# Differential attention: the next head's maxima and exponentials stand ahead of this head's mixing and copy

## The reference

```python
def one_block(args):
    a1, a2, i = args
    q_chunk = (i * Q_BLOCK + jnp.arange(Q_BLOCK)) // CHUNK
    mask = (key_chunk[None, :] <= q_chunk[:, None])[None, None]
    s1 = jnp.einsum('bqhd,bkhd->bhqk', a1, k1) * scale
    s2 = jnp.einsum('bqhd,bkhd->bhqk', a2, k2) * scale
    p1 = jax.nn.softmax(jnp.where(mask, s1, -jnp.inf), axis=-1)
    p2 = jax.nn.softmax(jnp.where(mask, s2, -jnp.inf), axis=-1)
    p = (p1 - lam * p2)
    return jnp.einsum('bhqk,bkhe->bqhe', p, v)
...
o = rmsnorm_2(o, b_subln[j], SUBLN_EPS) * (1.0 - lam_init)
x = x + concat([o, memory_attention]) @ w_o[l]
```

## Time and profile before

| | before |
|---|---|
| median of 3 runs | 1191.41 us (1191.03 to 1191.85) |
| the profiled execution's own time | 1190.21 us |
| its span, first to last instruction | 1188.4 us |
| mean granted TensorE clock | 0.947 of full |
| PE busy | 1109.9 us (93%) |
| DVE busy | 641.9 us (54%) |
| ACT busy | 534.8 us (45%) |
| POOL busy | 356.4 us (30%) |
| stretch of the six heads, 918.09 to 964.04 us | 45.95 us, of it PE busy 32.55 us, granted clock 0.68 |

### The profile page before, as it was taken

The page is one execution under the profiler, slowest core; times in us unless marked ns, Lnnn a source line. Parts: engine busy times, 40 slices in busy tenths (PEclk is TensorE's granted clock), DMA queues, the critical chain, the costliest instruction groups (busy, mean ns, idle before and its releaser), DMA issues.

```text
span 1188.4 us, 20203 instructions
## 1 busy us (share of the span) xinstructions
PE 1109.9 (93%) x8758; PEld 1083.8 (91%) x8758; DVE 641.9 (54%) x833; ACT 534.8 (45%) x737; POOL 356.4 (30%) x198
## 2 busy tenths in 40 slices
PE   7989999999899999959998999999998668999998
PEld 7989989889899999959998999998997558999998
DVE  2767766455575744464744544444646644644443
ACT  3337756664356544334344443443534432544441
POOL 3233726514054622111013221231531121323111
PEclk9879989989899999979998999998999688999999
DMA  9857755844547655524354655564442103655640
GB/s 321 242 188 221 246 178 156 270 143 142 178 138 252 210 191 189 192 71 142 107 179 129 202 189 190 178 200 142 142 142 72 36 19 98 203 178 180 187 166 36
DMA packets 167716, 197.39 MB, mean 166 GB/s; under 512 B 5283, under 2 KB 139852, under 8 KB 167500
## 3 DMA queue, kind: packets, MB, share of 16 engines
q1 hardware_dynamic: 167628, 196.11, 51.4%
HBM read 195.03 MB, written 1.06 MB: 165 GB/s over the span
## 4 chain that ended last, share of the span: by engine, by line
PE 75%; DVE 10%; ACT 7%; DMA 3%; POOL 2%; issue 2%; DVEq 0%; SPq 0%; ACTq 0%; POOLq 0%
PE bank L459 74%; DVE w_lo L1433 3%; DMA ada_raw<-in_w_ada 3%; ACT w_hi L974 2%; ACT ada_raw L964 2%; ACT probs L1020 1%; POOL ada_raw L1312 1%; POOL root L1288 1%; DVE fresh L1469 1%; DVE fresh L1475 0%; DVE ada_late L1749 0%; DVE y_tok L1527 0%; DMA qk<-in_mem 0%; POOL head_bias L1350 0%; DVE big L1631 0%
## 5 line engine op out<-in xcount | busy, mean ns | idle before, releaser
L1433 DVE TENSOR_TENSOR w_lo<-w_raw,w_hi 128x2048 fp32r<-128x2048 f32 x158 | 386.5, 2449 | 301.3 <-ACT w_hi L974 300.4
L459 PE MATMUL bank<-h_hi,w_hi 128*128 128x256 f32 x1328 | 383.6, 294 | 14.6 <-ACT h_hi L983 10.2
L459 PE MATMUL bank<-h_hi,w_lo 128*128 128x256 f32 x1328 | 378.9, 290 | 0.0
L974 ACT ACTIVATE w_hi<-w_raw 128x2048 fp32r<-128x2048 f32 x158 | 301.2, 1907 | 132.7 <-PE bank L459 132.6
L459 PE MATMUL bank<-h_lo,w_hi 128*128 128x256 f32 x1328 | 345.1, 285 | 0.0
L459 PE MATMUL bank<-u_hi,w_hi 128*128 128x256 f32 x1056 | 301.6, 289 | 8.8 <-DVE xT L1826 4.6
L459 PE MATMUL bank<-u_hi,w_lo 128*128 128x256 f32 x1056 | 298.9, 287 | 0.0
L459 PE MATMUL bank<-u_lo,w_hi 128*128 128x256 f32 x1056 | 285.5, 286 | 0.0
L459 PEld LDWEIGHTS bank<-h_hi,w_hi 128*128 128x128 f32 x1328 | 265.6, 200 | 18.5 <-issue 13.5
L1281 POOL TENSOR_TENSOR u_lo<-fresh,u_hi 128x512 fp32r<-128x512 f32 x68 | 153.6, 2262 | 425.2 <-ACT u_hi L983 425.0
L459 PEld LDWEIGHTS bank<-h_hi,w_lo 128*128 128x128 f32 x1328 | 265.3, 200 | 0.0
(11 more groups left out here) (188 smaller groups left out, 968.0 us busy)
## 6 DMA issues: line engine op xcount, KB each, us to landing
w_raw<-in_w_mlp SPq DMA_DIRECT2D x32, 1024.0 KB, 5.4
w_raw<-in_w_up SPq DMA_DIRECT2D x32, 1024.0 KB, 5.5
w_raw<-in_w_down SPq DMA_DIRECT2D x32, 1024.0 KB, 5.1
w_raw<-in_w_in SPq DMA_DIRECT2D x21, 1024.0 KB, 5.8
ada_raw<-in_w_ada SPq DMA_DIRECT2D x20, 1024.0 KB, 8.1
w_raw<-in_a_w_in SPq DMA_DIRECT2D x10, 1024.0 KB, 5.1
w_raw<-in_w_o SPq DMA_DIRECT2D x8, 1024.0 KB, 5.2
w_raw<-in_w_kv SPq DMA_DIRECT2D x6, 1024.0 KB, 4.9
```

The lines of the kernel that those rows point to most:

```text
L459: return pe.matmul(dst, lhsT, rhs, start=start, stop=stop, skip_group_check=True)
L974: act.activation(w_hi[:, n % PARTS_RING, :], w_raw[:, slot_of[n], :], ACT.Copy).then_inc(hi_w, 1)
L1433: dve.tensor_tensor(w_lo[:, n % PARTS_RING, :], w_raw[:, slot_of[n], :], w_hi[:, n % PARTS_RING, :].bitcast(F32), ALU.subtract).then_inc(l ...
```

## The change

On VectorE `d_maxima(h + 1)` moves from behind `o_mean(h - 1)` to the head of the turn, ahead of `mix(h)`; `o_scale(h - 1)` then follows `o_mean(h - 1)` directly. On ScalarE `d_exps(h + 1)` moves to the head of the turn, ahead of the wait for the transposes and the copy of head h. TensorE's and GpSimd's lists are the same, no instruction is added or taken away, and no wait is added or dropped.

```diff
@@ ScalarE
             for h in range(DIFF_HEADS):
+                if h + 1 < DIFF_HEADS:
+                    d_exps(h + 1)
                 act.wait_ge(d_turned, h + 1)
                 if h >= 2:
                     act.wait_ge(misc_full, misc_no[f"pv{h - 2}"] + 1)
                 act.activation(probsT[:, h % 2, 0:384], ps_ada[:, 0:384], ACT.Copy).then_inc(d_copied, 1)
-                if h + 1 < DIFF_HEADS:
-                    d_exps(h + 1)
                 if h >= 3 and h % 2:
                     split_h(J_DIFF + h // 2 - 1, u_hi, h - 3)
@@ VectorE
             for h in range(DIFF_HEADS):
+                if h + 1 < DIFF_HEADS:
+                    d_maxima(h + 1)
                 mix(h)
                 if h >= 2:
                     o_take(h - 2)
                 if h >= 1:
                     o_mean(h - 1)
-                if h + 1 < DIFF_HEADS:
-                    d_maxima(h + 1)
-                if h >= 1:
                     o_scale(h - 1)
                 o_copy(h)
```

## The result

The changed kernel takes 1206.18 us (median of 4 runs, 1205.86 to 1207.96); the kernel before, measured beside it, 1191.22 us (4 runs, 1188.78 to 1191.85). The ratio is 1.0136, with a 95% interval of 1.0121 to 1.0151: 1.4% slower, 15 us. The profiled execution has a span of 1204.2 us instead of 1188.4.

A forecast was written before the change was run, and what follows sets the result against it. TensorE was taken to bound the heads, with mixing hidden beside it; 3.20 us idle in each of turns 1 to 4 plus half clock in turns 2 to 4 gave +18.1 on 1191.41, 1209.5 us; range 1200 to 1214.5.

The forecast's parts named there:

- rival 1: Turns 2 to 4: clock holds mostly full despite the same idle chain; +8.9 us, up to +13; 1200.3 to 1204; chance 0.23.
- What bounds the stretch: Six heads: TensorE sets the time; mixing runs hidden beside filler(h-1) and scores(h+1), and TensorE waits for it only twice.
- The chain, 3.20 us in each of turns 1 to 4: Before the transposes of head h: scores(h+1), maxima(h+1), mix(h) become serial, leaving TensorE idle 3.20 us per turn.
- Turns 0 and 5 not touched: Turn 0: maxima(1) fit into mix(0)'s 1.9 us wait; turn 5 has no maxima(6), its mixing stays beside filler(4).
- Rival 2: Half clock also over turn 5 and the last filler: +24.3 us, 1215.7; chance 0.08.
- Exponentials ahead of the copy cost nothing: ScalarE, each turn: the 1.87 us of exponentials finish before the copy of head h may start; loss taken as 0.
- The clock: Turns 2 to 4: half clock taken, with a short rise after filler(1), scores(3) taking 1.93 instead of 2.93 us; +18.1 us.
- The trace against the Trainium skill: Skill: short idle gaps leave the clock full; prediction objected that half clock came after turn 4's 1.67 us gap.
- o_mean directly ahead of o_scale: VectorE sits out the round trip to GpSimd (0.69 us); between 0 and 0.3 us a turn, taken as 0.
- the collision: Head 4: L1914, 1.56 us beside the GpSimd split, would run undisturbed after the change; about 1 us more if they met.
- Rival 3: Turn 4: earlier exponentials remove the 1.67 us wait and the fall of the clock; -3.8 us, 1187.6; chance 0.03.
- rival 4: Behind the heads: the delay meets a slack, so the change does nothing that can be seen; chance 0.03.

The follow-up runs named there:

- dve_only: Kernel before with only VectorE's half: maxima of head h+1 ahead of the mixing of head h, ScalarE unchanged; 1208.06 us, ratio 1.0148.
- one_turn: Kernel before with the change made in turn 2 only, all other turns as before; 1195.20 us, ratio 1.0041.
- scores_early: Changed kernel with TensorE's scores(h+2) moved directly behind the transposes of head h, ahead of pv(h); 1195.79 us, ratio 1.0043.
- act_only: Kernel before with only ScalarE's half: exponentials of head h+1 ahead of the copy of head h, VectorE unchanged; 1205.11 us, ratio 1.0123.
- the kernel with extra work: Changed kernel with 10 unused constant multiplications between scores(h+1) and the wait for the mixing in turns 1 to 4; 1199.63 us, ratio 1.0079.
- early_fillers: Kernel before with the fillers of turns 1 and 2 moved into turn 0, ahead of the first transposes; 1190.51 us, ratio 0.9997.
- before_warm: Kernel before with extra unused constant multiplications put where TensorE idles in the heads; 1186.32 us, ratio 0.9962.

## Why the prediction was right

Forecast 1209.5 us, range 1200 to 1214.5, slower with 0.94; measured 1206.2. The change was to be +18.1 us and is +15.0. That is at the lowest edge of the forecast's own range (1206 to 1214), 2 us above the upper end of rival 1.

- *What bounds the stretch.* Right. The mixing of head h had been hidden beside filler(h-1) and scores(h+1), and lost that cover. It is shown by dve_only (all of the loss), one_turn (one turn, one price) and scores_early (the price falls when the scores stand elsewhere).
- *The chain, 3.20 us in each of turns 1 to 4.* Measured 3.21 four times. Less the 1.67 us that head 4 had waited before, 11.1 us predicted and 11.24 found.
- *Turns 0 and 5 not touched.* Right: head 0's transposes wait 4.8 us as before, those of head 5 not at all. Rival 2 (turn 5 and the filler behind it at half clock) did not show: from the output transposes of turn 5 to the end of the stretch both kernels take 4.59 us.
- *Exponentials ahead of the copy cost nothing.* Right for the change, with the condition that act_only shows: only since the maxima are early as well.
- *The clock.* The right mechanism, the wrong size. I took the half clock for turns 2 to 4 but for one short rise: 12.07, 10.60 and 12.95 us. Measured 11.25, 8.87 and 12.96, at 0.69, 0.84 and 0.50. The clock rose twice, in scores(3) right behind filler(1) and in the middle of filler(2) (a matmul of 128x256 goes from 0.41 to 0.28 us at 953.4), and the second rise lasted through scores(4) and the transposes of head 3, over an idle time of 3.21 us. The clock term was to be 7.0 us (18.1 less 11.1) and is 4.3; that is nearly the whole miss of 3 us. The measured +15.0 us lies between the case of half clock and rival 1 (+8.9, with part of the turns at half up to +13): turns 2 and 3 went partly its way, turn 4 as forecast. The prediction had no rule for when a turn keeps the clock, and these runs don't settle one.
- *The trace against the Trainium skill.* Turn 3 kept the full clock over a 3.21 us gap (the three transposes behind it take 0.55 us), turn 2 lost it in a gap of the same length (0.90 us). The rule of the Trainium skill, page "TensorE: Matmul & The Clock Gate", section "Why this matters for your kernels", that short gaps leave the clock and long ones take it, does not tell these two apart, nor does my use of the 1.67 us of turn 4 against it.
- *o_mean directly ahead of o_scale, and the collision.* The step missed a victim. The split L1281 no longer met L1914 in head 4, as predicted, but met L1940 in turn 3, the instruction that the change had moved there:

```profile
960.42 1.56 DVE L1940 TENSOR_SCALAR y_tok<-y_tok,stat 128x128 f32<-128x128 f32 x2 [0.81 <-POOL stat L1413]
```

  It takes 0.48 us elsewhere. The split began at 960.64. The price here was 0.07 us (the output transposes waited 0.65 instead of 0.58 us), since at half clock pv covered it; in the kernel with extra work, at the full clock, the same transposes waited 1.34 us.
- *Rival 3 (faster) and rival 4 (a slack behind the heads).* Neither showed: the transposes of head 4 wait 3.21 us instead of 1.67, and the `xT` wait is 4.6 us in both kernels.

## What to carry to other kernels

When an instruction is moved ahead of another on an in-order engine, its wait moves with it: ask what the producer of its input still has to do, and whether the consumer of the displaced instruction stands right behind that producer. Here TensorE stood at both ends, and work that cost nothing beside it became 3.2 us of idle time in each of four turns. Before filling idle time with work taken from elsewhere, ask what that work did for the clock where it was.

## What the runs showed of the hardware

- The busy share of a stretch does not settle its clock. Turn 3 of the kernel before ran at 1.00 with TensorE busy 3.33 of 4.58 us (73%); the same turn in early_fillers ran at 0.50, busy 6.00 of 7.25 (83%), behind turns without a filler. What ran before it differs, its own work does not. (At half the clock the same matmuls are busy longer, so the share is higher for that reason alone.)
- A matmul whose result nobody uses can pay: 39 extra calls of 0.25 to 0.46 us, in gaps of 0.6 to 5 us, took 4 us off the program (1186.3 us against 1190.1, before_warm).
- A VectorE `TENSOR_SCALAR` pair from SBUF to SBUF that takes 0.48 us took 1.56 beside a GpSimd `TENSOR_TENSOR`, wherever the two met: L1914 in heads 0 and 4 of the kernel before, L1914 in head 0 and L1940 in turn 3 of the changed one. The copy L1925 out of PSUM kept its 0.49 us beside such a split in the kernel before (963.30, with the split from 962.81 to 964.07).
